# The linear recurrence's gates moved from the delta net's opening into the last RWKV round, and six banks for the opening's first tiles

## The reference

```python
xc = causal_depthwise_conv(u, conv_w) + conv_b
r = sigmoid(einsum('btni,nij->btnj', xh, w_a) + b_a)      # xh: xc in 16 blocks of 64
i = sigmoid(einsum('btni,nij->btnj', xh, w_x) + b_x)
log_a = (-LRU_C * r) * softplus(-lam)
a = exp(log_a)
b = sqrt(-expm1(2.0 * log_a)) * (i * xc)
h_t = a_t * h_{t-1} + b_t                                 # associative scan over time
y_a = h * gelu(gate)
```

## Time and profile before

| | |
|---|---|
| median of 3 runs | 3193.99 us (3192.87 to 3194.53) |
| the profiled execution | 3198.14 us |
| its span, from the first to the last instruction | 3196.3 us |
| mean granted TensorE clock | 0.997 |
| busy: PE, DVE, ACT, POOL | 98%, 71%, 54%, 9% |
| DMA | 434.94 MB, mean 136 GB/s |

### The profile page before, as it was taken

The page is one execution under the profiler, slowest core; times in us unless marked ns, Lnnn a source line. Parts: engine busy times, 40 slices in busy tenths (PEclk is TensorE's granted clock), DMA queues, the critical chain, the costliest instruction groups (busy, mean ns, idle before and its releaser), DMA issues. The chain is left out here.

```text
span 3196.3 us, 73397 instructions
## 1 busy us (share of the span) xinstructions
PE 3122.3 (98%) x24736; PEld 2763.7 (86%) x24736; DVE 2262.7 (71%) x4909; ACT 1720.8 (54%) x3662; POOL 286.8 (9%) x270
## 2 busy tenths in 40 slices
PE   8999999999999999999999999999999999999998
PEld 7899888889897888888888888888899978888887
DVE  6777576667886677777677775766678766777776
ACT  6665454432495555555565564443425955555555
POOL 1322211110000000000022321111000000000000
PEclk9999999999999999999999999999999999999999
DMA  4332232223225555555442322322432265555554
GB/s 156 102 102 89 95 106 99 92 100 146 99 72 174 189 189 185 195 184 190 171 143 80 108 75 102 116 93 88 145 114 88 66 196 186 195 184 191 190 185 163
DMA packets 122814, 434.94 MB, mean 136 GB/s; under 512 B 15808, under 2 KB 18112, under 8 KB 122048
## 3 DMA queue, kind: packets, MB, share of 16 engines
q1 hardware_dynamic: 122688, 433.31, 39.1%
HBM read 432.21 MB, written 1.05 MB: 136 GB/s over the span
## 5 line engine op out<-in xcount | busy, mean ns | idle before, releaser
L2581 PE MATMUL bank<-x_both,u_parts 128*128 128x512 f32 x1536 | 557.9, 397 | 0.8 <-DVE u_parts L2691 0.8
L2565 PE MATMUL bank<-v_parts,act_high 128*128 128x512 f32 x1024 | 404.9, 395 | 3.7 <-DVE v_parts L2521 2.1
L2567 PE MATMUL bank<-v_parts,act_low 128*128 128x512 f32 x1024 | 399.8, 390 | 0.0
L2577 PE MATMUL bank<-x_both,u_parts 128*128 128x256 f32 x1536 | 399.6, 281 | 0.0
L2566 PE MATMUL bank<-v_parts,act_high 128*128 128x512 f32 x1024 | 398.8, 389 | 0.0
L2691 DVE TENSOR_TENSOR u_parts<-u_raw,u_parts 128x512 fp32r<-128x512 f32 x384 | 265.6, 692 | 184.6 <-ACT u_parts L2634 182.2
L353 PE MATMUL bank<-x_parts,w_parts 128*128 128x256 f32 x1248 | 388.8, 312 | 1.6 <-DVE w_parts L338 1.1
L2521 DVE TENSOR_TENSOR v_parts<-v_raw,v_parts 128x512 fp32r<-128x512 f32 x512 | 330.2, 686 | 34.9 <-ACT v_parts L2516 33.2
L354 PE MATMUL bank<-x_parts,w_parts 128*128 128x256 f32 x1248 | 352.0, 282 | 0.0
L355 PE MATMUL bank<-x_parts,w_parts 128*128 128x256 f32 x1248 | 351.7, 282 | 0.0
L2634 ACT ACTIVATE u_parts<-u_raw 128x512 fp32r<-128x512 f32 x384 | 242.4, 632 | 187.1 <-PE bank L2581 147.1
(11 more groups left out here) (386 smaller groups left out, 6254.7 us busy)
## 6 DMA issues: line engine op xcount, KB each, us to landing
v_raw<-in_v SPq DMA_DIRECT2D x256, 512.0 KB, 3.5
u_raw<-in_u SPq DMA_DIRECT2D x192, 512.0 KB, 4.1
ring<-in_w_side SPq DMA_DIRECT2D x80, 512.0 KB, 3.6
ring<-in_w_gdn SPq DMA_DIRECT2D x64, 512.0 KB, 3.5
ring<-in_w_rwkv SPq DMA_DIRECT2D x46, 512.0 KB, 3.6
ring<-in_w_gdn_side SPq DMA_DIRECT2D x32, 512.0 KB, 3.5
ring<-in_u SPq DMA_DIRECT2D x32, 512.0 KB, 3.9
u_ring<-in_u SPq DMA_DIRECT2D x32, 512.0 KB, 3.4
```

Of the source, the lines that this page charges most:

```text
L2565: te.matmul(ps, f32r(w_hi), f32r(x_hi), start=start, stop=False, **kw)
L2567: return te.matmul(ps, f32r(w_lo), f32r(x_hi), start=False, stop=stop, **kw)
L2577: return te.matmul(banks[r % 4][:, T:2 * T], f32r(u_lo[:, cols]), f32r(xhigh[:, k]), start=False, stop=stop)
L2581: mm = te.matmul(banks[r % 4][:, :].rearrange("p (x t) -> p x t", x=2), f32r(u_hi[:, cols]), f32r(x_both[:, :, k]), start=(k == 0), stop=( ...
```

## The change

The sixteen gate products, their sigmoids, the rates (softplus of lambda) and the logs leave the opening. The products (`gate_products`) take the place of the turns in the last RWKV round: in banks 0 and 1, four in level one and three in each other, each from the third on waiting for the sigmoid of the same gate one block before. Level one's first also waits for f1's taps. ACT's fills of that round take the sigmoids; `scalar_rates` stands on ACT ahead of f1's eviction, `vector_rates_first` on DVE ahead of the taps, `vector_rates` behind `bv` and ahead of the levels, and three logs behind each chunk's R add. SP issues the parameters and gate weights in round 0. The arena's regions are rearranged so that the gates' results lie where the RWKV block's dead tiles were. In the opening, PE begins with alpha and beta and goes on to the tiles, of which the first six have six banks and the last two wait for the taps six before; the recurrence's functions and the decays are put in another order among the tiles. The reading of tiles by ACT and DVE goes by `ps_of(s, i)` too, and the regions of `gdn_phase` are cut here. Lines removed from `Lru` stand in the listing above.

```diff
--- before
+++ after
@@ -394,104 +394,94 @@
 class Lru:
...
+    def __init__(self):
         self.V, self.S, self.E = steps("lru_vec"), steps("lru_act"), steps("lru_pe")
         self.pload = lru_params
         self.par, self.wax = gdn_made.lru_par, gdn_made.lru_gates
...
+        self.small = gdn_made.lru_small
+        r = Region(LRU_GATES_AT)
+        self.rr, self.ii = r(KT, T), r(KT, T)
+        self.gates_end = r.at_
+        r = Region(LRU_DECAYS_AT)
+        self.aa, self.bb = r(KT, T), r(KT, T)
         self.c = {n: k for k, n in enumerate(LRU_COLS)}
...
+    def gate_products(self, te, first, n):
         S, E = self.S, self.E
...
+        for m in range(first, first + n):
+            k, x = divmod(m, 2)
+            if k:
+                te.wait_ge(S.sem, S.at("ri"[x] + str(k - 1)))
+            te.matmul(banks[x][:, 0:T], self.wax[:, k, x, :], yb[:, k, :], start=True, stop=True)\
+                .then_inc(E.sem, E.one("ri"[x] + str(k)))
+    def gate_sigmoids(self, a, first, n):
+        S, E, c = self.S, self.E, self.c
+        for m in range(first, first + n):
+            k, x = divmod(m, 2)
+            bias = c[("ba", "bx")[x]]
+            a.wait_ge(E.sem, E.at("ri"[x] + str(k)))
+            a.activation((self.rr, self.ii)[x][:, k, :], banks[x][:, 0:T], ACT.Sigmoid, bias=self.par[:, k, bias:bias + 1])\
+                .then_inc(S.sem, S.one("ri"[x] + str(k)))
+    def scalar_rates(self, a):
         a.wait_ge(self.pload, 32)
         a.wait_ge(self.V.sem, self.V.at("neg"))
         softplus_exp(a, self.S, self.small[0], self.small[1], "sp")
...
+    def vector_rates_first(self, v):
+        v.wait_ge(self.pload, 32)
+        v.tensor_scalar(self.small[0], self.par[:, :, self.c["lam"]], -1.0, None, ALU.mult).then_inc(self.V.sem, self.V.one("neg"))
+    def vector_rates(self, v):
+        v.wait_ge(self.S.sem, self.S.at("sp_e"))
+        v.wait_ge(self.V.sem, self.V.now())
+        softplus_log(v, self.V, *self.small)
+        v.wait_ge(self.V.sem, self.V.now())
+    def vector_logs(self, v, ks):
+        V, S, spl, rr = self.V, self.S, self.small[4], self.rr
+        for k in ks:
+            v.wait_ge(S.sem, S.at(f"r{k}"))
+            v.tensor_scalar(rr[:, k, :], rr[:, k, :], spl[:, k:k + 1], LRU_C, ALU.mult, ALU.mult).then_inc(V.sem, V.one(f"nla{k}"))
+    def scalar(self, a, tile, decays, rates):
+        V, S, rr, aa, bb = self.V, self.S, self.rr, self.aa, self.bb
+        a.wait_ge(V.sem, V.at(f"nla{KT - 1}"))
         a.activation(bb, rr, ACT.Tanh).then_inc(S.sem, S.one("tanh"))
+        a.activation(aa, rr, ACT.Exp, scale=-1.0).then_inc(S.sem, S.one("a"))
+        decays()
         tile(0)
...
         a.wait_ge(S.sem, S.now())
         a.activation(rr, rr, ACT.Exp, scale=-2.0).then_inc(S.sem, S.one("a2"))
...
+        tile(1)
         a.wait_ge(V.sem, V.at("b2"))
         a.activation(bb, bb, ACT.Sqrt).then_inc(S.sem, S.one("b"))
+        tile(2)
+        a.activation(ya, ya, ACT.Gelu_apprx_tanh).then_inc(S.sem, S.one("gelu"))
         tile(3)
...
+        rates()
+        for n in range(4, 8):
+            tile(n)
+    def vector(self, v, tile, decays):
         V, S, rr, ii, aa, bb = self.V, self.S, self.rr, self.ii, self.aa, self.bb
...
+        v.wait_ge(S.sem, S.at(f"i{KT - 1}"))
         v.tensor_tensor(ii, ii, yb, ALU.mult).then_inc(V.sem, V.one("ix"))
...
+        decays()
+        v.wait_ge(S.sem, S.at("a2"))
+        v.scalar_tensor_tensor(bb, rr, 1.0, bb, ALU.add, ALU.mult).then_inc(V.sem, V.one("b2"))
         tile(0)
         tile(1)
...
         v.wait_ge(S.sem, S.at("b"))
         v.wait_ge(V.sem, V.now())
         for n in range(2):
             ks = slice(n * KT // 2, (n + 1) * KT // 2)
             v.tensor_tensor(bb[:, ks], bb[:, ks], ii[:, ks], ALU.mult).then_inc(V.sem, V.one("bx"))
...
+        tile(2)
+        for k in range(KT):
+            if k == 4:
                 tile(3)
...
             v.wait_ge(V.sem, V.now())
             v.tensor_tensor_scan(rr[:, k, :], aa[:, k, :], bb[:, k, :], 0.0, ALU.mult, ALU.add)\
                 .then_inc(V.sem, V.one("scan"))
@@ -499,10 +489,8 @@
         v.wait_ge(V.sem, V.now())
+        tile(4)
+        tile(5)
@@ -564,7 +552,9 @@
 GDN_ROOM = MIXER - 8 * 12 - 1 - KT * 16 - 32
-LRU_ROOM = GDN_ROOM - KT * len(LRU_COLS) - KT * 2 * P
+LRU_ROOM = GDN_ROOM - KT * len(LRU_COLS) - KT * 2 * P - 6 * KT
+LRU_GATES_AT = BRANCH + KT * (len(RWKV_COLS) + len(RWKV_MADE) + len(LRU_COLS)) + 3 * KT + 2 * P + 4 + 3 * T
+LRU_DECAYS_AT = LRU_GATES_AT + 2 * KT * T + 8 * T
 class GdnParams:
@@ -573,17 +563,21 @@
         self.lru_par, self.lru_gates = r(KT, len(LRU_COLS)), r(KT, 2, P)
+        self.lru_small = [r(KT) for _ in range(6)]
...
+lru = Lru()
+def lru_first_loads(sp, l):
+    sp.dma_start(gdn_made.lru_par, A["lru_par"][l]).then_inc(lru_params, 16)
+    sp.dma_start(gdn_made.lru_gates, A["lru_gates"][l]).then_inc(lru_params, 16)
 def gdn_first_loads(sp, l):
...
     sp.dma_start(gdn_made.nw, A["gdn_norm"][l]).then_inc(gdn_params, 16)
-    sp.dma_start(gdn_made.lru_par, A["lru_par"][l]).then_inc(lru_params, 16)
-    sp.dma_start(gdn_made.lru_gates, A["lru_gates"][l]).then_inc(lru_params, 16)
@@ -657,8 +651,11 @@
     Z = r_(3, T)
+    assert r_.at_ == LRU_GATES_AT
     WA, SG = r_(T), r_(T)
-    (kkr, sq, sg, cs, cm, Pm, Pp, Pi, rs, aa, kk, kf, kp, rk, nb, NBt, KH, bv, gt, y) = (r_(T) for _ in range(20))
+    (kkr, sq, sg, cs, cm, Pm, Pp, Pi, rs, aa, kk, kf, kp, nb) = (r_(T) for _ in range(14))
+    assert r_.at_ == lru.gates_end
+    (rk, NBt, KH, bv, gt, y) = (r_(T) for _ in range(6))
     KR = r_(NB, 2, P)
@@ -736,6 +733,7 @@
             first_side(1)
+            lru_first_loads(sp, l)
             with sp.Fori(1, NI - 1) as i:
@@ -844,6 +842,10 @@
             v.tensor_tensor(KR[:, :, 0], two(kk), two(Pm), ALU.mult).then_inc(VA.sem, VA.one("KR"))
+        def lru_part(lev, *ys):
+            before = 0 if lev == 1 else 3 * lev - 2
+            return before + 2 * ys[0], sum(2 if lev == 1 or y == 0 else 1 for y in ys)
         def pe_side(te, i, what, ks, more):
@@ -851,9 +853,9 @@
                     elif what == "f0":
-                        te.wait_ge(*((VA.sem, VA.at("shift1", i + 1)) if more else (VF.sem, VF.at("tap3", i))))
+                        te.wait_ge(*((VA.sem, VA.at("shift1", i + 1)) if more else (lru.S.sem, lru.S.at(f"i{KT - 1}"))))
                     elif what == "f2":
-                        te.wait_ge(*((VA.sem, VA.at("shift2", i + 1)) if more else (SF.sem, SF.before("f4", i))))
+                        te.wait_ge(*((VA.sem, VA.at("shift2", i + 1)) if more else (lru.S.sem, lru.S.at(f"r{KT - 1}"))))
                     else:
@@ -948,10 +950,12 @@
                     pe_piece(te, i + 1, 2 * lev + y)
-                elif lev and (y == 0 or lev == 5):
-                    if lev == 1:
+                elif lev:
+                    if (lev, y) == (1, 0):
                         te.wait_ge(SF.sem, SF.before("f4", i))
-                    turn(te, ps_in[0], 2)
+                        te.wait_ge(VF.sem, VF.at("tap3", i))
+                        te.wait_ge(lru.pload, 32)
+                    lru.gate_products(te, *lru_part(lev, y))
                 if more and (lev, y) == (5, 1):
@@ -1119,6 +1123,11 @@
             def fill(n):
+                if not more:
+                    if n == 1:
+                        a.wait_ge(E.sem, E.at("gate", i))
+                        a.wait_ge(VA.sem, VA.at("KR", i))
+                    lru.gate_sigmoids(a, *lru_part(n, 0, 1))
                 if more and n == 1:
@@ -1154,6 +1163,8 @@
                 act_round(a, i + 1, "r")
+            else:
+                lru.scalar_rates(a)
             act_side(a, i, 1)
@@ -1269,11 +1280,15 @@
                 vec_rest(v, i + 1, "r")
+            else:
+                lru.vector_rates_first(v)
             vec_taps(v, i)
...
                 vec_rest(v, i + 1, "k")
+            else:
+                lru.vector_rates(v)
             v.wait_ge(S.sem, S.at("invT", i))
@@ -1289,6 +1304,8 @@
                     v.tensor_tensor(Rs[rows], b5[rows, 0:P], AVO[rows, b], ALU.add).then_inc(V.sem, V.one(f"R{q}"))
+                    if not more:
+                        lru.vector_logs(v, range(3 * q - 3, min(3 * q, KT)))
                     if q == 1 and more:
@@ -1514,6 +1537,8 @@
         ps_a = [banks[(s + 1) % 2][:, 0:T] for s in range(8)]
+        ps_first = [banks[n][:, 0:T] for n in (1, 0, 4, 5, 7, 6, 1, 0)]
+        ps_of = lambda s, i: (ps_first if isinstance(i, int) and i == 0 else ps_a)[s]
         ps_g = [banks[n % 2][:, 0:T] for n in range(4)]
@@ -1521,12 +1546,14 @@
                         te.wait_ge(loaded[s % 4], 16 * (s // 4) + 16)
-                    if s >= 2:
+                    if first and s >= 6:
+                        te.wait_ge(VA.sem, VA.at(f"tap3_{s - 6}", i))
+                    elif s >= 2 and not first:
                         te.wait_ge(VA.sem, VA.at(f"tap3_{s - 2}", i))
...
                 if first:
```

(37 more changed lines are left out.)

120 lines of the change are left out of this document (16 added, 104 removed).

## The result

The change makes the kernel slower: 3204.43 us against 3195.85 us for the kernel before (medians of 16 runs each), with a ratio of 1.0021 on record, 95% interval 1.0015 to 1.0028 (the quotient of the two medians is 1.0027). The forecast was 3188.9.

The account below looks back on a forecast made before the run. PE, busy 98%, was taken to bound the kernel. Openings -17.7, last rounds +12.0 and queue +0.6 sum to -5.1 us, giving a median of 3188.9 us; range 3183.0 to 3194.8.

Parts of the forecast that it names:

- The opening: Delta net's start: gate products and the waits for a bank and `ya` go, saving 8.85 us per layer, 17.7 in all.
- The logs: Chunk loop: logs lie in DVE's idle time behind each R add, costing nothing; without that cover 2.4 us a layer.
- C: Opening: the clock does not fall there, a further 4.5 us gained, 3184.4 us; chance 0.10.
- F: Opening: DVE's chain (taps of tile six, or `ya`) ends it, not PE; 1.5 us a layer, 3191.9; chance 0.08.
- G: Opening: the tiles' loads pace it and half of what went is waited for instead, 3197.7 us; chance 0.04.
- D: Last round: the clock falls in level 1 and stays low through the levels, 3203 us; chance 0.08.
- B: Last round: it costs only PE's own time, 6.8 us in all, giving 3183.7 us; chance 0.12.
- E: Table loads: each of the four new ones costs double, +5.1 us, giving 3194.0 us; chance 0.03.
- the queue: Round 0: `rwkv_up` is issued 1.0 us later, lands in 5.6 us; PE waits 0.3 us per layer, 0.6 in all.
- level one: Last round's first level: table loads, later taps, sigmoids and softplus_log delay the next product by 2.7 us per layer.
- levels two to five: Last round: gate products waiting for sigmoids add 0.93 us in each of levels 2 to 4, 0.5 in level 5.
- the clock: Opening: low clock costs the same 4.5 us in both layers together as before, so no term.

Follow-up runs that it names:

- e9: Changed kernel with the recurrence's loads moved to the last round, gate products through four banks, and Abs and Exp ahead of round 0: 3203.53 us, ratio 1.0023.
- e2: Changed kernel with negation, Abs and Exp of the rates ahead of round 0 and the softplus behind level two's add: 3207.48 us, ratio 1.0036.
- e8: Changed kernel with Abs reading lambda itself in the last round, so ACT does not wait for the negation: 3201.54 us, ratio 1.0016.
- e0: The changed kernel run again, unchanged, beside the kernel before: 3204.38 us, ratio 1.0027.
- e3: Changed kernel with the gate products through four banks, each waiting for the sigmoid two blocks back: 3198.79 us, ratio 1.0008.
- e7: Changed kernel with only Abs and Exp moved ahead of round 0, behind the decays, Abs reading lambda itself: 3200.25 us, ratio 1.0015.
- e11: Changed kernel with loads moved to the last round, gate products through four banks, and Abs reading lambda itself in the last round: 3190.63 us, ratio 0.9979.

## Why the prediction was wrong, step by step

**Right.** The opening: 8.85 us a layer forecast, 9.04 and 10.71 measured. Of the 19.75 us, 1.7 are clock: 1.7 and 3.4 lost before, 1.7 in each layer after; the other 18.05 answer to 17.7. Its parts hold: the body's releaser is z7's eviction, DVE's taps end 1.1 us ahead of it, the clock falls in both layers. The logs lie in DVE's idle time, and nothing of the chunk loop moved. Rivals C, F and G fell with that. D did not come about: the levels keep the full clock in both layers; e9, with a gap of 3.1 us, and e2, with gaps of 1.8, show that it could have. B fell with the steps of 3.75 us. So did E: Exp's load at 360.61 is over at 361.89 and the next activation starts at 361.91 with no drain, and e8 hides the load whole.

**Wrong: the queue, +0.6 forecast, +4.8 measured.** The step that failed is "it lands like the slowest of fourteen, in 5.6 us": PE could start only 6.5 and 6.7 us behind the issue, and 6.9 and 7.3 in e0. The issue itself moved "by 1.0" as forecast in layer 1 and in both layers of e0; only in layer 0 of this profile, where SP spent 1.23 us on the 1 MB of gates, did it move by 1.8 in the round (2.3 in the whole). With the landing of 6.5 to 7.3 us the wait is 1.4 to 1.9 us a layer, beyond the end given, 1.3. What I did not cost at all is the clock behind such a wait: 1.7 us in layer 0.

**Wrong: level one, +2.7 forecast, +4.2 measured.** Two links failed. "ACT's new Abs waits for `neg` on DVE, which is free at 355.8": DVE was free when the forecast said (the negation starts 3.42 us behind the Gram products, 355.8 is 3.5 behind them), but the sum gives the negation no time of its own, and it takes 0.73 us beside GpSimd's L1432. ACT sat idle 2.47 us and f1 moved 1.7, not 1.2. And "Behind the level's copy on ACT (about 359.6) comes a load back to the Sigmoid table": the load starts behind the wait for the product, not ahead of it, so it lay whole on the path (PE's 1.49 us). The last link, the end of `softplus_log` and the add behind it, was held to be the bound; it ended 1.16 us ahead of the add. It became the bound once PE's wait for the second load was gone (e3, e7, e9, e11).

**Mis-sized: levels two to five, +3.3 forecast, +4.1 measured.** The mechanism is as forecast, steps of 3.75 where 3.44 was said. e3 shows what is in it: 0.85 a level is PE's own time, 0.4 the wait for the sigmoid in a shared bank.

**Put at nothing: the clock.** The step was "I take the same 4.5 us in both layers together, so no term", and nothing outside the opening. The clock falls in a few places (the opening, round 0 here, at 640 and 2220), and each fall costs 1.7 us or two or three times that. Of the 2.0 us that the rest of layer 0 takes more, 1.7 are such a fall at 640, behind narrow products (128x1); the profile of before has the same products and no fall there, and of the thirteen profiles of changed kernels only e9's has none. In the opening the loss was 5.1 us before and 3.4 after in both layers together, and up to 10.2 in the same code (e8). Over the runs the changed kernel loses more: beside e0 the mean granted clock is 0.9958 in ten runs, and 0.9977 in 26 of the kernel before, which makes an estimated 6 of the 9 us by which their mean spans differ. Why it falls more often is open. By span less loss the change lies 1.8 us above the kernel before, and e11 9.0 below it.

## What to carry to other kernels

Work moved into a stage full of small waits costs what it adds to each hand-over on top of its busy time: give it banks of its own, so that it waits for nobody. A wait added to an engine is costed up to the end of the producer's work, with the time that this work takes where it will stand (0.73 us here for a step of 0.16 elsewhere), not by when that engine is free; ask first whether the operand is needed at all (Abs of a negation). A small transfer put behind a large one is costed with a landing of its own, not with the slowest seen without the large one. And where a repair lets one engine run ahead, look at what it then releases: in e9 the removal of two table loads was paid for by GpSimd's work meeting VectorE's.

## What the hardware showed that was not expected

- Single 128x8 steps of VectorE take 0.17 us alone; some that met a GpSimd instruction took 0.73 to 1.28 us (L434 here, L376 and L380 in e2, L389 and L392 in e9), and the end of that instruction ends them. Not every step that meets one stands: L378 in e2 took 0.21.
- The opening takes 32.3 us plus what the clock costs, and that came as 1.7, 3.4 or 5.1 us, in the same code: 34.05, 35.7 and 37.33. Why a run gets the one or the other was not settled.
- Behind PE's waits of 1.91 us in round 0 and 3.10 us in e9, both in layer 0, the clock fell to the 1.2 GHz level for a while; behind those of 1.37 and 3.13 us in layer 1 of the same kernels it did not. The length of a wait does not tell: it fell behind 1.66 us in e7 and not behind 2.40 in e2, both in round 0 of layer 0.
- Tanh ran here without a load behind Sigmoid's table: behind the last round the opening needs no load for it, but Exp needs one (1.28 us at 405.99, beside PE's work).
